# Expert stage of a two-block layer: gathered rows replaced by dense products over both tables

## The chip, the cores and the metric

One core of a Trainium2 chip runs the whole program. The metric is the device time of one execution in microseconds; times of the kernel before are the median of three runs. TensorE is called PE in the profile, its weight loads PEld, VectorE DVE, ScalarE ACT, GpSimd POOL, and SP is the queue that issues most transfers.

## What is computed

Two transformer-like blocks over 256 tokens of width 1024, all in f32. The part that the change rewrites is the expert layer at the end of the first block. It has 16384 experts, each with one row of 1024 numbers in a table u and one in a table v (64 MB a table). For each token, 8 heads pick 16 experts each by products of two half keys, 128 experts in all, with softmax gates:

```python
def chunk(args):
    xc, ec, gc = args
    u = expert_u[ec]
    act = jax.nn.gelu(jnp.einsum('cd,ced->ce', xc, u).astype(jnp.float32))
    return jnp.einsum('ce,ced->cd', gc * act, expert_v[ec])
```

The expert index is i1 * 128 + i2, where i1 and i2 are the winners of the two half-key searches. Before this layer stand modulation vectors, an attention with three branches, a short convolution and the output projection; behind it a residual add, a norm, and the whole second block (attention, a gated delta rule, gates, output projection, norm).

## The kernel before

The tokens are two tiles of 128. Every engine has its own instruction queue, written out in order by the Python program (`PE`, `V`, `A`, `G`, `SP` are TensorE, VectorE, ScalarE, POOL and SP); an engine runs its queue strictly in that order and each entry names the earlier results that it waits for (`after`). Nearly every instruction is recorded under one line, L87, so groups are told apart by the tiles that they name. PSUM has eight banks of 128x512, handed out in turn by `ps.take()`. Weights of 1024x512 come in 2 MB loads into four slots `W`, in the order of the list `plan` (line 160 on): `next_w` takes the next, `done_w` releases it and asks for the block four places on.

`attn_mm(a)` is the output projection of token tile a (16 products of 512 columns), `attn_add(a)` its residual add on VectorE, `queries(a)` the norm, the transposes (`norm_T`), the query projection (64 products of 128 columns), and, back in token order, the row `tok2[:, a]` that the gathers need. `key_scores` gives the half-key scores; `route(a)` (line 780) picks top 16 by repeated max operations on VectorE, in tiles `RT`, `PT` and `acc`, and ends in the expert index `idx` and the gate `gw`. It is a generator: its instructions are put into VectorE's queue a few at a time, between those of the gathers.

The expert stage is the loop `for m in range(17)` (line 959). Block m is 16 experts of one head of a token tile. For each expert slot s, POOL issues an indirect transfer that fetches for each of the 128 tokens its own row of table u (512 KB) into one of 14 buffers of `AR`. VectorE multiplies it with the token's row and sums into `av`. Sixteen such sums go through gelu and the gates to `wv`. One block later POOL fetches the v rows of the same slots; ScalarE makes a diagonal matrix of the 128 weights, and TensorE multiplies it with the rows into two PSUM banks `E[a]` (two products of 512 columns for each slot). That is 2 x 256 fetches. In between stand `mod_row(3, n)` (a gate row of the modulation, 16 products of 512 columns in all), the route of tile 1, and from m = 8 on for token tile 0, whose sums are complete by then: `x2(0)` (gate, residual, norm), the second block's norm and transposes, `qk_project` (q and k, four times 8 products of 512 columns) and `rope`. After the loop the same is done for tile 1, and the second block goes on with `rope_turn`, the projections of tile 1 and of v, and so on.

## Time and profile before

| | us |
|---|---|
| median of three runs | 1529.59 |
| lowest and highest | 1529.15, 1543.69 |
| span of the profiled execution | 1593.7 |
| mean granted TensorE clock in it | 0.944 |

The span is from the first instruction to the last in one execution with the profiler on. Busy time of an engine is that of its compute instructions; a matmul's end is modelled and overlaps the next one's start a little, so for dense stretches the step from one start to the next tells the cost. An f32 product shows as two MATMUL records, and two weight loads. "Idle before" is what stood ahead of the instructions of a group, with the releaser that ended it.

### The profile page before, as it was taken

To read this page: it belongs to the slowest core of one execution; us is meant where nothing else is said; L and a number is where in the kernel's file an instruction comes from. 1 tells how busy PE (TensorE), PEld (TensorE's weight loads), DVE (VectorE), ACT (ScalarE), POOL (GpSimd) and SP (SyncE) were. 2 spreads that over 40 slices of the span, in tenths; PEclk is the share of its full clock that TensorE was granted. 3 is DMA by queue.
4 is the path that set the end of the run, shared out by engine and by line. 5 is a ranking of instruction groups with operands and counts; after the bars stand their busy time and mean duration, and the time that the engine had idled before them with its cause. 6 is when DMAs were issued, how large, how long until landed. Compare 5 with 4: busy or idle time off the path is not lost.

```text
span 1593.7 us, 12966 instructions
## 1 busy us (share of the span) xinstructions
PE 1283.0 (81%) x4744; PEld 769.3 (48%) x4744; DVE 750.8 (47%) x1673; ACT 335.6 (21%) x725; POOL 660.3 (41%) x541
## 2 busy tenths in 40 slices
PE   5899878757767777638887877779998698999896
PEld 1697536622322232213333322244676478999783
DVE  2223544778775854435444444320367764441211
ACT  1031211121110121102111111120486452111101
POOL 0787000767777776766777777710000000000000
PEclk9889788889999999988999999989999999999998
DMA  9775300999999999997999999934432131114120
GB/s 341 268 265 211 106 14 1 347 404 370 367 353 370 368 387 388 373 357 256 362 374 361 375 346 394 366 144 160 162 117 92 53 106 53 53 53 157 55 106 26
DMA packets 127690, 376.94 MB, mean 237 GB/s; under 512 B 10403, under 2 KB 12620, under 8 KB 127564
## 3 DMA queue, kind: packets, MB, share of 16 engines
q0 software_dynamic: 73728, 268.47, 44.6%
q1 hardware_dynamic: 52112, 103.46, 18.1%
q10 hardware_dynamic: 1788, 4.19, 0.8%
q8 instruction: 38, 0.62, 0.2%
q14 instruction: 24, 0.20, 0.0%
HBM read 375.02 MB, written 1.06 MB: 236 GB/s over the span
## 4 chain that ended last, share of the span: by engine, by line
PE 41%; DVE 17%; DMA 15%; POOL 13%; issue 7%; ACT 5%; another core or an unknown queue 2%; SPq 0%; DVEq 0%; ACTq 0%
PE ps L87 41%; POOL AR L87 13%; DMA AR<-in_pv,idx 9%; DVE AR L87 7%; DMA AR<-in_pu,idx 3%; ACT L87 2%; DMA W<-in_w_mod 2%; DVE acc L87 2%; DVE RT L87 2%; DVE tok L87 1%; ACT AR L87 1%; DVE hT L87 1%; DVE junk L87 1%; DVE PT L87 1%
## 5 line engine op out<-in xcount | busy, mean ns | idle before, releaser
L87 PE MATMUL ps<-AR,acc 128*128 128x512 f32 x1024 | 502.5, 626 | 173.2 <-DMA AR<-in_pv,idx 116.9
L87 DVE CUSTOM_DVE_ANT_0 AR<-AR,tok 128x1024 f32<-128x1024 f32 x256 | 312.1, 1222 | 263.0 <-DMA AR<-in_pu,idx 227.0
L87 PEld LDWEIGHTS ps<-AR,acc 128*128 128x128 f32 x1024 | 183.6, 194 | 490.3 <-DMA AR<-in_pv,idx 246.3
L87 POOL DMA_INDIRECT AR<-in_pu,idx x256 | 269.5, 1053 | 215.6 <-DVE hred L87 124.9
L87 POOL DMA_INDIRECT AR<-in_pv,idx x256 | 298.8, 1167 | 109.2 <-issue 57.8
L87 PE MATMUL ps<-hT,W 128*128 128x256 f32 (+2 forms) x1504 | 320.7, 372 | 7.0 <-issue 2.4
L87 PEld LDWEIGHTS ps<-hT,W 128*128 128x128 f32 (+1 forms) x1504 | 270.2, 196 | 50.7 <-issue 12.8
L87 ACT ACTIVATE acc<-K,wv 128x128 f32<-128x128 f32 x256 | 86.9, 393 | 227.9 <-PE ps L87 137.0
L87 ACT ACT_TABLE_LOAD x87 | 111.6, 1283 | 16.7 <-issue 15.2
L87 PE MATMUL ps<-W,hT 128*128 128x512 f32 (+3 forms) x288 | 95.1, 487 | 0.0
L87 PE MATMUL ps<-K,tok 128*128 128x128 f32 x128 | 28.2, 390 | 52.7 <-DVE tok L87 52.7
L87 PEld LDWEIGHTS ps<-W,hT 128*128 128x128 f32 x288 | 48.0, 190 | 45.1 <-issue 45.0
L87 POOL TENSOR_TENSOR W<-W,st 128x4096 f32<-128x4096 f32 x6 | 42.1, 7014 | 61.7 <-DMA W<-in_w_mod 61.7
L87 ACT ACTIVATE wv<-av 128x16 f32<-128x16 f32 x16 | 3.4, 215 | 264.3 <-issue 172.8
L87 PE MATMUL ps<-AR,W 128*128 128x256 f32 x256 | 57.1, 379 | 0.0
L87 PEld LDWEIGHTS ps<-K,tok 128*128 128x128 f32 x128 | 22.7, 205 | 62.5 <-DVE tok L87 53.3
L87 ACT ACTIVATE AR<-ps 128x512 f32<-128x512 f32 (+5 forms) x53 | 24.2, 471 | 128.9 <-PE ps L87 128.9
L87 PEld LDWEIGHTS ps<-AR,W 128*128 128x128 f32 x256 | 48.2, 190 | 6.3
L87 PE MATMUL ps<-AR 64*64 64x30 f32 (+4 forms) x288 | 47.6, 312 | 1.0 <-DVE rowb L87 1.0
L87 ACT ACTIVATE PT<-ps 128x512 f32<-128x512 f32 x34 | 19.8, 591 | 118.2 <-PE ps L87 118.2
L87 PEld LDWEIGHTS ps<-AR 64*64 64x64 f32 (+2 forms) x288 | 39.0, 197 | 9.1 <-issue 4.9
L87 POOL TENSOR_TENSOR W<-W 128x2048 f32<-128x2048 f32 (+1 forms) x12 | 41.7, 3478 | 0.9
(200 smaller groups left out, 1035.9 us busy)
## 6 DMA issues: line engine op xcount, KB each, us to landing
W<-in_w_in SPq DMA_DIRECT2D x25, 2048.0 KB, 7.8
W<-in_w_mod SPq DMA_DIRECT2D x12, 2048.0 KB, 16.2
W<-in_w_out SPq DMA_DIRECT2D x2, 2048.0 KB
W<-in_wq SPq DMA_DIRECT2D x2, 2048.0 KB, 10.5
AR<-in_pu,idx POOLq DMA_INDIRECT x256
AR<-in_pv,idx POOLq DMA_INDIRECT x256
W<-in_wba SPq DMA_DIRECT2D x2, 2048.0 KB, 7.9
W<-in_wbb SPq DMA_DIRECT2D x2, 2048.0 KB, 7.8
```

Of the source, the lines that this page charges most:

```text
L87: ins = f(*args, **kw)
```

## The change

The routing stays, but for its cut: `route` now puts all its instructions out in three goes, for four heads at a time, and keeps i1 and i2 (`i12`) rather than the index. In place of the gathers:

- Both tables are laid out on the host in 64 blocks of 1 MB, each of a pair of blocks of 128 experts. SP's queue loads block after block into a ring of four buffers. The ring lies where weight slots 0 and 1 are.
- `act_pair(p)`: products of the u block with all 256 tokens, 2 x 8 products of 256 columns into one bank; ScalarE's gelu writes the result (expert by token) into `held`, 128 x 256 numbers for each partition. It covers the gather buffers and, by the time that they are needed, slots 2 and 3 and the tiles `tok2`, `acc`, `mixT`, `PT`, `RT`.
- The gates of a token over all experts are a 128 x 128 matrix, the product of two one-hot matrices of 128 columns (i2, made by POOL; i1 times the gate, made by VectorE) over the 128 chosen. `one_hots(g)` makes them for four tokens, `gate_mm(g)` multiplies (4 products of 128 columns), `gate_spread(g)` multiplies them into those experts of `held` that are there, and ScalarE copies the rest, for which `gate_pair` multiplies later. Two such groups go with each pair from 30 to 61.
- The second table, from pair 28 on and round: for each block 2 x 2 x 2 products of 512 columns, `held` times v, into four banks.

Also moved: `attn_mm(1)` ahead of `queries(0)`, `mod_row(3, n)` ahead of `attn_add(1)`, the transposes back to token order are gone, and tile 0's `x2`, norm, transposes and q and k projections now follow the whole expert stage. Weight blocks 22 to 25 of the plan are loaded late: 22 and 23 in the second table's pass, 24 and 25 after its last product. Rows 0 and 1 of `rowb` are loaded after the gate products.

```diff
+M_W23 = M_AR + 14 * D
+M_TOK = M_W23 + 2 * 4096
+M_ACC = M_TOK + 2 * D
...
         def done_w(i, tok):
-            load_w(i + NSLOT, [tok])
+            if not L1 - NSLOT <= i < L1:
+                load_w(i + NSLOT, [tok])
...
-        for r in range(4):
+        for r in (2, 3):
             SP.dma(nc.sync.dma_start, s_row, rowb[:, r, :], rows[r, :].partition_broadcast(P))
         t_row = SP.dma(nc.sync.dma_start, s_row, abb[:, :], ab[0, :].partition_broadcast(P))
...
-            for k4 in range(2):
-                b = ps.take()
-                for kk in range(4):
-                    t = PE(tr, b.t[:, kk * 128:kk * 128 + 128], hT[:, 4 * k4 + kk, c], ident, after=b.old + t_h)
-                e = A(act, tok2[:, a, k4 * 512:k4 * 512 + 512], b.t[:, :], ACT.Copy, after=[t, t_xn])
-                b.free = [e]
-                t_h2[a].append(e)
+            t_h2.extend(t_h)
+            t_tp2.append(t_xn)
...
-        attn_add(0, attn_mm(0))
+        ob0, ob1 = attn_mm(0), attn_mm(1)
+        attn_add(0, ob0)
         queries(0)
-        RT = sb("RT", [P, 6 * 256])
+        t_g2 = [mod_row(3, n) for n in range(2)]
+        attn_add(1, ob1)
+        queries(1)
...
-        ob1 = attn_mm(1)
-        routes = [route(0, kb, [stage[7, "O"]])]
-        while (0, 0) not in t_idx or (0, 0) not in t_gw:
-            advance(routes[0], 1)
-        attn_add(1, ob1)
-        queries(1)
...
-        def fetch(table, a, s):
-            n = gn[0] % NGB
-            gn[0] += 1
-            return n, G.dma(nc.gpsimd.indirect_dma_start, gsem[n], GB[:, n, :], None, table,
-                            bass.IndirectOffsetOnAxis(ap=idx[:, a, s:s + 1], axis=0),
-                            after=slot_free[n] + [t_idx[a, s // 16]])
...
+        ring = [M[:, r * 2048:r * 2048 + 2048] for r in range(4)]
+        rsem = [dsem(f"s_r{r}") for r in range(4)]
+        turn_v = [*range(28, NPAIR), *range(28)]
+        t_ring = []
+        def fetch(i, after):
+            if i < 2 * NPAIR:
+                src = pu[i, :, :] if i < NPAIR else pv[turn_v[i - NPAIR], :, :]
+                t_ring.append(SP.dma(nc.sync.dma_start, rsem[i % 4], ring[i % 4], src, after=after))
+        for i in range(4):
+            fetch(i, [t_g2[i // 2]])
+        ones2 = held.rearrange("p (c t) -> p c t", t=S)
+        t_act, t_prod, t_store, t_one = {}, {}, {}, {}
...
+        def act_pair(p):
+            b = ps.take()
+            u = ring[p % 4].rearrange("p (k e) -> p k e", k=8)
+            for cc in range(2):
+                for k in range(8):
+                    t = PE(mm, b.t[:, cc * 256:cc * 256 + 256], u[:, k, cc * 128:cc * 128 + 128], hT[:, k, :],
+                           start=(k == 0), stop=(k == 7), after=b.old + [t_ring[p]] + t_h2)
+            fetch(p + 4, [t])
+            src = b.t[:, :].rearrange("p (c t) -> p c t", c=2)
+            dst = ones2[:, 2 * p:2 * p + 2, :]
+            n = min(8 * max(p - P0, 0), S)
+            b.free = []
+            if n < S:
+                e = A(act, dst[:, :, n:], src[:, :, n:], ACT.Gelu_apprx_tanh, after=[t] + t_tp2)
+                b.free.append(e)
+            if n:
+                e = A(act, src[:, :, 0:n], src[:, :, 0:n], ACT.Gelu_apprx_tanh, after=[t])
+            t_act[p] = e
+            return b, src, dst, n
+        def gate_pair(p, b, src, dst, n):
+            if n:
+                t_prod[p] = V(tt_, dst[:, :, 0:n], src[:, :, 0:n], dst[:, :, 0:n], MUL,
+                              after=[t_act[p], t_store[2 * (n // 8) - 1]])
+                b.free.append(t_prod[p])
+        def one_hots(g):
+            h = hot[g % 3]
+            for j in range(4):
+                c = 4 * g + j
+                t2_ = G(nc.gpsimd.tensor_scalar, h[:, 0, j, :], i128, i2T[:, c:c + 1], None, ALU.is_equal,
+                        after=hotfree[g % 3] + t_turned)
+                t = V(ts_, h[:, 1, j, :], i128, i1T[:, c:c + 1], gT[:, c:c + 1], ALU.is_equal, MUL,
+                      after=hotfree[g % 3] + t_turned)
+            t_one[g] = [t, t2_]
+        def gate_mm(g):
+            b = ps.take()
+            h = hot[g % 3]
+            for j in range(4):
+                t = PE(mm, b.t[:, j * 128:j * 128 + 128], h[:, 0, j, :], h[:, 1, j, :], start=True, stop=True,
+                       after=b.old + t_one[g])
+            hotfree[g % 3] = [t]
+            return b, t
+        def gate_spread(g, b, t):
+            c = 2 * (P0 + g // 2 + 1)
+            src = b.t[:, :].rearrange("p (t c) -> p c t", t=4)
+            dst = ones2[:, :, 4 * g:4 * g + 4]
+            t = V(tt_, dst[:, 0:c, :], src[:, 0:c, :], dst[:, 0:c, :], MUL, after=[t, t_act[P0 + g // 2]])
+            b.free = [t]
+            t_prod["g"] = t
+            if c < P:
+                t = A(act, dst[:, c:, :], src[:, c:, :], ACT.Copy, after=[t])
+                b.free = [t]
+            t_store[g] = t
+        def turn_route(a):
+            b = ps.take()
+            for n, src in enumerate((i12[:, 0, :], i12[:, 1, :], gw[:, a, :])):
+                t = PE(tr, b.t[:, n * 128:n * 128 + 128], src, ident, after=b.old + [t_i12[a], t_gw[a]])
+            c = slice(a * 128, a * 128 + 128)
+            e = A(act, junk[:, 512:1024].rearrange("p (c t) -> p c t", c=2)[:, :, c],
+                  b.t[:, 0:256].rearrange("p (c t) -> p c t", c=2), ACT.Copy, after=[t] + t_jx[-1:])
+            e = A(act, gT[:, c], b.t[:, 256:384], ACT.Copy, after=[t])
+            b.free = [e]
+            return t, e
+        routes = route(0, kb, [stage[7, "O"]], [])
+        kb1 = []
+        for p in range(P0):
+            act_pair(p)
+            if p == 5:
+                next(routes)
+                kb1.append(key_scores(1, 0))
+            if p == 13:
+                next(routes)
+                next(routes)
+                t_turn0, e0 = turn_route(0)
+                kb1.append(key_scores(1, 1))
+                routes = route(1, kb1, [t_gw[0]], [t_turn0])
+            if p == 20:
+                next(routes)
+            if p == P0 - 2:
+                next(routes)
+                next(routes)
+                t_turned = [e0, turn_route(1)[1]]
+        one_hots(0)
+        one_hots(1)
+        for p in range(P0, NPAIR):
+            pair = act_pair(p)
+            gs_ = [g for g in (2 * (p - P0), 2 * (p - P0) + 1) if g < NPAIR]
+            banks = [gate_mm(g) for g in gs_]
+            for g, (b, t) in zip(gs_, banks):
+                if g + 2 < NPAIR:
+                    one_hots(g + 2)
+                gate_spread(g, b, t)
+            gate_pair(p, *pair)
+        s_row2 = dsem("s_row2")
+        for r in range(2):
+            t_row2 = SP.dma(nc.sync.dma_start, s_row2, rowb[:, r, :], rows[r, :].partition_broadcast(P),
+                            after=hotfree[0] + hotfree[1])
+        E = [[ps.take(), ps.take()] for _ in range(2)]
+        for q, p in enumerate(turn_v):
+            v = ring[q % 4].rearrange("p (c d) -> p c d", c=2)
+            for cc in range(2):
+                for a in range(2):
+                    for n in range(2):
+                        t = PE(mm, E[a][n].t[:, :], ones2[:, 2 * p + cc, a * 128:a * 128 + 128],
+                               v[:, cc, n * 512:n * 512 + 512], start=(q == 0 and cc == 0),
+                               stop=(q == NPAIR - 1 and cc == 1),
+                               after=E[a][n].old + [t_ring[NPAIR + q], t_act[p], t_prod["g"], t_store[NPAIR - 1]]
+                               + ([t_prod[p]] if p in t_prod else []))
+            fetch(NPAIR + q + 4, [t])
+            if q == 15:
+                load_w(L1, [t])
+                load_w(L1 + 1, [t])
+        load_w(L1 + 2, [t])
+        load_w(L1 + 3, [t])
+        t_pelast = t
...
-        for m in range(17):
-            last = None
-            for s in range(16):
-                if m < 16:
-                    a, h = blocks[m]
-                    q = h * 16 + s
-                    n, t = fetch(pu, a, q)
-                    last = V(ttr, GB[:, n, :], GB[:, n, :], tok2[:, a, :], 1.0, 0.0, MUL, ADD, av[:, a, q:q + 1],
-                             after=[t] + t_h2[a])
-                    slot_free[n] = [last]
-                    t_last0 = last if a == 0 else t_last0
-                    t_last1 = last
-                if m >= 1:
-                    a, h = blocks[m - 1]
-                    q = h * 16 + s
-                    n, t = fetch(pv, a, q)
-                    if q == 0:
-                        E[a] = [ps.take(), ps.take()]
-                    d = dn[0] % NDG
-                    dn[0] += 1
-                    td = A(act, dg[:, d, :], ident, ACT.Copy, scale=wv[:, a, q:q + 1], after=[t_w[m - 1]] + dg_free[d])
...
-                        routes = [route(1, [key_scores(1, 0), key_scores(1, 1)], [t_idx[0, 7], t_gw[0, 7]])]
-            if m in (4, 5):
-                t_g2.append(mod_row(3, m - 4))
-            if m < 16:
-                a, h = blocks[m]
-                c = slice(h * 16, h * 16 + 16)
-                t = A(act, wv[:, a, c], av[:, a, c], ACT.Gelu_apprx_tanh, after=[last])
-                t_w[m] = V(tt_, wv[:, a, c], wv[:, a, c], gw[:, a, c], MUL, after=[t, t_gw[a, h]])
-            if m == 8:
-                assert (1, 7) in t_gw
-                t_x2[0] = x2(0, e, [])
-                t_xb = norm_x(0, st[:, 16:17], [t_x2[0]], tok2, [t_last0])
-                t_, t_tp = norm_T((0,), tok2, [t_xb], PV[:, V_PRE:V_PRE + 8], None, [])
-                t_hb.append(t_)
-            if m in (9, 10):
-                qk_project("qk"[m - 9], 0, 0, [t_tp, t_gw[1, 7]])
...
-        t_x2[1] = x2(1, t_pelast, t_rot["k", 0])
-        t_xb = norm_x(1, st[:, 17:18], [t_x2[1]], tok2, [t_last1])
-        t_, t_tp = norm_T((1,), tok2, [None, t_xb][1:], PV[:, V_PRE:V_PRE + 8], None, [])
+        t_x2[0] = x2(0, t_pelast, [])
+        t_xb0 = norm_x(0, st[:, 16:17], [t_x2[0]], tok2, [t_pelast])
+        t_, t_tp0 = norm_T((0,), tok2, [t_xb0], PV[:, V_PRE:V_PRE + 8], None, [])
         t_hb.append(t_)
+        t_x2[1] = x2(1, t_pelast, [t_xb0])
+        t_xb = norm_x(1, st[:, 17:18], [t_x2[1]], tok2, [t_pelast])
+        for n in range(2):
+            for kind in "qk":
+                qk_project(kind, 0, n, [t_tp0])
+        t_, t_tp = norm_T((1,), tok2, [t_xb], PV[:, V_PRE:V_PRE + 8], None, [])
+        t_hb.append(t_)
+        rope("q", 0, [t_xb])
+        rope("k", 0, t_rot["q", 0])
         t_hball = t_hb[0] + t_hb[1]
         at[0] = 0
...
+    pu = a["peer_u"][0].reshape(NPAIR, 2 * P, 8, P).transpose(0, 3, 2, 1).reshape(NPAIR, P, 2 * D)
+    pv = a["peer_v"][0].reshape(NPAIR, 2, P, D).transpose(0, 2, 1, 3).reshape(NPAIR, P, 2 * D)
```

## Rows read from the trace of the kernel before

**Rows 1.** The page, parts 1 and 3: engines' busy time; the gathers' queue.
```profile
PE 1283.0 (81%) x4744; PEld 769.3 (48%) x4744; DVE 750.8 (47%) x1673; ACT 335.6 (21%) x725; POOL 660.3 (41%) x541
q0 software_dynamic: 73728, 268.47, 44.6%
```
**Rows 2.** Busy by stretches: length; PE, PEld, DVE, ACT, POOL; clock, DMA share, GB/s.
```profile
330.00:1060.00 730.00, 548.02 (x1160) 206.01 (x1160) 389.94 (x884) 108.00 (x296) 530.71 (x483) 0.96 0.96 360
```
**Rows 3.** Groups by shape, whole span (busy, mean ns, idle before); POOL's first gather.
```profile
L87 PE MATMUL ps<-AR,acc 128*128 128x512 f32 x1024 | 502.5, 626 | 173.2 <-DMA AR<-in_pv,idx 116.9 <-issue 37.0 <-ACT acc L87 19.0
L87 DVE CUSTOM_DVE_ANT_0 AR<-AR,tok 128x1024 f32<-128x1024 f32 x256 | 312.1, 1222 | 263.0 <-DMA AR<-in_pu,idx 227.0 <-issue 35.9
...
L87 POOL DMA_INDIRECT AR<-in_pu,idx x256 | 269.5, 1053 | 215.6 <-DVE hred L87 124.9 <-issue 69.2 <-DVE av L87 10.9
...
280.25 1.11 POOL L87 DMA_INDIRECT AR<-in_pu,idx  x1 [124.88 <-DVE hred L87]
```
**Rows 4.** TensorE in order of time, first output projection to key scores.
```profile
229.63 15.67 PE L87 MATMUL ps<-W,mixT 128*128 128x512 f32 x32 [4.64 <-DVE modc L87]
249.30 1.97 PE L87 MATMUL ps<-K,tok 128*128 128x128 f32 x8 [4.00 <-DVE tok L87]
252.26 9.99 PE L87 MATMUL ps<-hT,W 128*128 128x128 f32 x64 [0.99 <-ACT hT L87]
...
264.57 7.41 PE L87 MATMUL ps<-hT,W 128*128 128x128 f32 x64
272.67 1.71 PE L87 MATMUL ps<-PT,mixT 64*128 64x128 f32 x16 [0.69 <-ACT mixT L87]
```
**Rows 5.** TensorE in order of time, end of the gathers and what follows.
```profile
1030.53 29.75 PE L87 MATMUL ps<-AR,acc 128*128 128x512 f32 x68 [0.58 <-issue]
1068.75 3.67 PE L87 MATMUL ps<-K,tok 128*128 128x128 f32 x16 [8.47 <-DVE tok L87]
...
1073.73 41.37 PE L87 MATMUL ps<-W,hT 128*128 128x512 f32 x96
```
**Rows 6.** TensorE in dense stretches, in order of time; one weight-load group by shape.
```profile
1427.26 1.95 PE L87 MATMUL ps<-tok,junk 128*128 128x128 f32 x16
1429.04 1.95 PE L87 MATMUL ps<-tok,PT 128*128 128x128 f32 x16
...
1434.29 7.07 PE L87 MATMUL ps<-hT,W 128*128 128x256 f32 x32
1441.19 7.07 PE L87 MATMUL ps<-AR,W 128*128 128x256 f32 x32
...
1553.80 27.70 PE L87 MATMUL ps<-W,acc 128*128 128x512 f32 x64 [1.60 <-DVE acc L87]
...
L87 PEld LDWEIGHTS ps<-W,acc 128*128 128x128 f32 x64 | 12.1, 190 | 16.8 <-issue 16.8
```
**Rows 7.** Busy time of a dense stretch, columns as in rows 2.
```profile
1434.00:1480.00 46.00, 46.00 (x264) 41.81 (x263) 7.17 (x11) 7.31 (x23) 0.00 (x0) 1.00 0.39 138
```
**Rows 8.** Busy time of the routing tile RT alone; PE, PEld, DVE, ACT.
```profile
240.00:1060.00 820.00, 0.00 (x0) 0.00 (x0) 118.36 (x472) 0.00 (x0) 0.95 0.91 343
```
**Rows 9.** The page, part 6: weight loads, KB each, us to landing.
```profile
W<-in_w_in SPq DMA_DIRECT2D x25, 2048.0 KB, 7.8
```
**Rows 10.** Groups by shape, whole span: nearest rows to the new small operations.
```profile
L87 POOL TENSOR_TENSOR W<-W 128x2048 f32<-128x2048 f32 x6 | 27.6, 4602 | 0.5
L87 POOL TENSOR_TENSOR mixT<-W 128x512 f32<-128x512 f32 x4 | 5.6, 1397 | 0.3
L87 POOL MEMSET AR<- 128x8 f32 x1 | 0.1, 106 | 0.0
...
L87 DVE TENSOR_SCALAR rowb<-rowb,sm 128x128 f32<-128x128 f32 x8 | 2.3, 287 | 0.3
L87 DVE TENSOR_TENSOR AR<-ps,bd 128x512 f32<-128x512 f32 x4 | 2.8, 692 | 7.7 <-PE ps L87 7.7
L87 ACT ACTIVATE PT<-ps 128x512 f32<-128x512 f32 x34 | 19.8, 591 | 118.2 <-PE ps L87 118.2
```

More of the change, by code:

```diff
@@ L777, in build, with route @@
         i16 = K[:, K_I16:K_I16 + 16]
-        t_idx, t_gw = {}, {}
-        def route(a, banks, hold):
+        t_gw = {}
+        t_i12 = {}
+        def route(a, banks, hold, hold_i):
             t_sel = hold
-            for h0, nh in ((0, 2), (2, 2), (4, 4)):
+            for h0, nh in ((0, 4), (4, 4)):
                 bs, t = banks[h0 // 4]
@@ L870, in route @@
-                yield
-                t_gn = V(tt_, g3, g3, hr.unsqueeze(2).to_broadcast([P, nh, 16]), MUL, after=[t])
-                for h in range(h0, h0 + nh):
-                    t_idx[a, h], t_gw[a, h] = t_new, t_gn
-                t_sel = t_sel + [t_new, t_gn]
-                yield
+            g3 = gw[:, a, :].rearrange("p (h s) -> p h s", h=8)
+            t = V(tt_, g3, t163[:, :, :], t163[:, :, 0:1].to_broadcast([P, 8, 16]), SUB, after=t_sel)
+            t_e = A(act, gw[:, a, :], gw[:, a, :], ACT.Exp, after=[t])
@@ L877, in advance @@
+            t = V(red, hred[:, a, :], g3, AX, ADD, after=[t_e])
+            t = V(rec, hred[:, a, :], hred[:, a, :], after=[t])
+            t_gw[a] = V(tt_, g3, g3, hred[:, a, :].unsqueeze(2).to_broadcast([P, 8, 16]), MUL, after=[t])
+            yield
         def advance(gen, n):
@@ new lines, in build @@
+        for i in range(4):
+            fetch(i, [t_g2[i // 2]])
+        ones2 = held.rearrange("p (c t) -> p c t", t=S)
+        t_act, t_prod, t_store, t_one = {}, {}, {}, {}
+        i1T, i2T = junk[:, 512:768], junk[:, 768:1024]
+        gT = sb("gT", [P, S])
+        i128 = K[:, K_I128:K_I128 + P]
+        hot = [rowb[:, r, :].rearrange("p (c t i) -> p c t i", c=2, t=4) for r in range(3)]
+        hotfree = [t_g1 + t_x1[1] for _ in range(3)]
+        def act_pair(p):
[17 more added lines that the diff above has]
+            return b, src, dst, n
@@ L920, in x2 @@
             t = rms(X[:, a, :], D, st[:, 14 + a:15 + a], [t])
-            return V(stt, X[:, a, :], X[:, a, :], st[:, 14 + a:15 + a], R_LNF, MUL, MUL, after=[t, t_row])
-        blocks = [(a, h) for a in range(2) for h in range(8)]
+            return V(stt, X[:, a, :], X[:, a, :], st[:, 14 + a:15 + a], R_LNF, MUL, MUL, after=[t, t_row2])
         rot = {("q", 0): tok2[:, 0, :], ("k", 0): acc[:, 1, :], ("q", 1): tok2[:, 1, :], ("k", 1): acc[:, 0, :]}
```

165 lines of the change are left out of this document (54 added, 111 removed).

## The prediction

> **What bounds the kernel now.** I read the page from the top. The first part says that no engine is busy for the whole span [rows 1]: an average over stages, so the stages were looked at next, by stretches. In the stretch of the gathers [rows 2] the 16 DMA engines are busy 0.96 of the time at 360 GB/s, TensorE 548.0 of 730 us, VectorE 389.9. The queue of the gathers moved 268.47 MB [rows 1], which is 512 fetches of 128 rows of 4 KB. The groups by shape say who waits: TensorE's products with gathered rows stand 173.2 us idle, 116.9 of them for gathered rows of the second table, VectorE's row products 263.0 us, 227.0 of them for rows of the first [rows 3]. So the stage ends when the rows are in. TensorE's last product with them ends at 1030.53 + 29.75 = 1060.3 [rows 5]. After that the kernel is a chain of TensorE, VectorE and ScalarE with hardly any DMA in it, and the change leaves that part as it is, but for its first few products.
>
> **What a product costs.** Every f32 product stands in the trace as two MATMUL records, a transpose as one. In dense stretches 32 records of 256 columns step by 1441.19 - 1434.29 = 6.90 us, 0.431 us a product; 16 records of 128 columns step by 1429.04 - 1427.26 = 1.78, 0.223 us a product; 64 records of 512 columns take 27.70 us, less about 0.17 for the last one's drain, 0.860 us a product [rows 6]. The granted clock was 1.00 in the first of these stretches [rows 7], which is the level of 2.4 GHz, so nothing is left to gain there.
>
> **The dense stage.** First table: 64 pairs of expert blocks, each 2 x 8 products of 256 columns, the very shape of the 32 records above: 64 x 6.90 = 441.6 us. Gate products: 256 (one per token) of 128 columns: 256 x 0.223 = 57.1. Second table: 64 x 2 x 2 x 2 = 512 products of 512 columns: 512 x 0.860 = 440.3 (439.6 by the last step of the records). Key scores of the second token tile (two blocks of 16 records, 1.64 each [rows 4]) 3.3, six turning transposes 0.7. Sum 942.3 us of TensorE alone; I take that for the stage, if TensorE never waits in it. What has to hide below it:
> - Tables: 1 MB per 6.9 us is 152 GB/s, against the 360 of the gathers [rows 2]. A load of 2 MB lands in 7.8 us [rows 9], and the ring of four asks for each block 20 us ahead. Hidden; it would cost only if the loads ran at less than half of what they do.
> - Routing: VectorE's work on the routing tile is 118.4 us for both token tiles [rows 8], some 59 each. The first must be through when TensorE, in order, comes to its transposes behind pair 13, 97 us after the stage's start, the second behind pair 28, 200 us after it. The next late thing would be TensorE itself, by whatever is missing. Hidden with 35 us to spare.
> - ScalarE: one activation of 128x512 for each pair (0.59 [rows 10]) and the copies of gates, under 1 us: under 2 of 6.9, with room for table loads.
> - One-hots and spreading, pairs 30 to 61: TensorE's own time there is 6.90 + 8 x 0.223 = 8.68 us a pair. VectorE has 8 tensor_scalar of 128x128 (0.287 each), two spreads and one product of 128x512 (0.692 each) [rows 10]: 4.4 us. POOL has 8 compares of 128x128, of which the trace has no row. From below 0.106 (8 columns), from above 1.397 (512 columns) [rows 10]; the step to 2048 columns (4.602) gives 2.1 ns a column and so 0.6 at 128, a line from the 8 columns gives 0.4. I take 0.5: 4.0 us a pair, hidden; at the upper end 11.2 a pair, not hidden (a rival below). The spread reads PSUM with a stride, of which I have no better row.
>
> A rule speaks against this. In rows, VectorE's and POOL's one-hots together are 2.3 + 4.0 = 6.3 us of 8.68 a pair, so even if they took turns the sum stays. The Trainium skill, "SBUF — State Buffer", section "Who interferes with whom", says that VectorE's tensor_scalar in its two-port mode and a POOL instruction lock each other out for a whole instruction. No row of before has the two side by side. By that rule with POOL's price at its upper end a pair would need 13.5 us and the kernel 1982 in place of 1909.
>
> **Ahead of the stage.** Before: first output projection 229.63 to 245.3, transposes at 249.30, query products 9.99 and 7.41, key scores 1.71 twice, and so on [rows 4]. After, TensorE's order is: both output projections, queries of tile 0, the gate row of w_mod (16 products, 13.7), queries of tile 1, the pairs. Tile 0: 245.3 + 13.7 (second projection) = 259.0; transposes 1.0 and eviction 1.0; then twice 7.4 + 0.7 + 1.6: 280.4. The gate row: 294.1, its add on VectorE (0.7) 294.8. Behind that add in VectorE's queue stand the residual adds of tile 1, and TensorE waits for them: four adds of 0.7 and the norm (the 4.00 us ahead of 249.30 less two adds, 2.6 [rows 4]) take it to 300.2; transposes and eviction 1.97 + 0.99, queries 9.99 + 7.4 (the first products at the lower clock, as in rows 4): 320.6. The stage then ends at 320.6 + 942.3 = 1262.9, that is 202.6 later than 1060.3.
>
> **Behind the stage.** In before the second normalization, the transposes and the projections of q and k for token tile 0 ran while gathers were awaited; only tile 1 stood behind. From 1060.3 the chain takes 8.47 us to the transposes and to 1073.73 for the next products, 13.4 in all [rows 5]. After, tile 0 comes first: 8.47, then 1.97 + 0.99, then four projections of 8 products of 512, 27.5 us, then tile 1's transposes with their eviction 2.0 (tile 1's own norm lies under the 27.5), the rotations of q and k, 12 small VectorE operations of 0.287 = 3.4, and transposes 0.9. That is 45.2, or 31.8 more. Two of the four weight blocks can only be asked for when the last table block is consumed; two loads of some 7.8 us, one behind the other, land at 16, and TensorE needs them at 8.5 + 3 + 13.7 = 25. Hidden.
>
> **Sum.** 1593.7 + 202.6 + 31.8 = 1828.1 us of span. Removed with the gathers: 512 issues on POOL (1.05 us each for the first table [rows 3]), 256 VectorE row products, 256 diagonals on ScalarE, 1024 MATMUL records; they lay beside one another in the 780 us from the first issue at 280.25 [rows 3] to 1060.3, whose end is compared above, and aren't subtracted again.
>
> **Span and time.** The profiled execution's span, 1593.7, is 64.1 us over the median of 1529.59. Where those 64 us sit decides what to set against the runs. The DMA engines were nearly full all through the gathers [rows 2]; a product at 512 columns in 0.43 us a record at full clock can't be faster in an undisturbed run. So I put all 64 into the gathers (0.125 us each of 512), which the change removes, and expect after's time at its span: 1828.
>
> **The rivals.**
> - *The 64 us are spread over the span.* Then the part that both kernels share, 1593.7 - 780 = 814 us, is 64.1 x 814 / 1593.7 = 33 shorter in undisturbed runs: 1795. For it: the DMA engines are at work outside the gathers too. Against: much of the rest is product-bound, and in the stretch of [rows 7] at the full clock. Chance 0.15.
> - *POOL's compares bound pairs 30 to 61.* At 1.397 each, 11.2 a pair against 8.68, 32 pairs: +81, 1909. It decides from 1.09 us each. For it: no row at 128 columns. Against: POOL's rows grow with the columns. Chance 0.10.
> - *The clock falls.* At the lower level (1.2 GHz) the first queries' 64 records of 128 columns took 9.99 against 7.41, the first few of them slow [rows 4]; a product stream at that level costs twice. In the first product alone: +442, 2270. Against: it fell only after TensorE had stood idle, and here it never does. Chance 0.04.
> - *The other side: a dense stream goes faster than the rows.* If a record cost only its weight load (0.190 [rows 6]) once the queue is full, the second table would cost 1024 x 0.190 = 195 (-245) and the first 2048 x 0.190 = 389 (-53): 1530, no change. It takes a saving of 299 out of 882 to decide. Against: 64 and 32 records on end already step at 0.43 and 0.216. Chance 0.03: 0.02 no change, 0.01 faster. The Trainium skill, "TensorE: Matmul & The Clock Gate", section "Back-to-back issue gap", has such a rule: it gives some 131 ns for a product of 512 columns in a real stream. By it the second table's 1024 records would be 134 us and the kernel 1522. The rows of this trace, at 430, contradict it.
>
> **How the numbers follow.** Forecast as summed, 0.68; the rivals 0.15, 0.10, 0.04, 0.03. The time is that of the likeliest, 1828. Its own range is 1810 to 1850 (the order ahead and behind, some 10 us each, and a few us around the span). The range down to 1785 takes in the spread of the 64 us, up to 1885 most of the way to POOL's bound. A measurement of this kernel can't tell less than about 1%; slower by over 1% has 0.97, same 0.02, faster 0.01.
>
> **What would show it.** In after: about 7168 MATMUL records of the expert stage, TensorE busy throughout at a granted clock of 1.00 between about 320 and 1263; DMA near 150 GB/s there; POOL's compares well under 1.09 us; transposes about 8.5 us behind the last product; the next chain 32 us longer than before. Wrong if TensorE has steady idle time in pairs 30 to 61 (named after POOL or VectorE), or if pairs take less than 6.9 us; and if after's time lies as far under its span as before's does, the 64 us weren't the gathers'.

## The result, and the profile after

The kernel after takes 1846.6 us (median of 4 executions, 1845.85 to 1847.62), the kernel before 1534.5 on the same chip; the ratio is 1.202, 95% interval 1.197 to 1.207. That is 19 us above the 1828 predicted, inside the predicted range and inside the forecast's own. The page of after:

```profile
span 1844.8 us, 17497 instructions
PE 1721.7 (93%) x7294; PEld 1226.7 (66%) x7294; DVE 547.8 (30%) x1456; ACT 290.9 (16%) x599; POOL 243.4 (13%) x285
PE 83%; DVE 10%; ACT 4%; DMA 2%; issue 1%; SPq 0%; DVEq 0%; ACTq 0%
M<-in_pv SPq DMA_DIRECT2D x64, 1024.0 KB, 4.9
```

The third line is the chain that ended last: 83% of it is TensorE. Against [rows 1] TensorE's busy share went from 81% to 93%, with 2550 records more (the stage's own products are 2048 + 512 + 1024 = 3584 records, and the 1024 with gathered rows are gone); the gathers' queue is gone, and each 1 MB table block lands in 4.9 us. The stretches, with the columns of [rows 2]:

```profile
540.00:780.00 240.00, 240.00 (x1322) 217.07 (x1321) 93.93 (x295) 34.77 (x108) 128.72 (x219) 1.00 0.35 123
830.00:1280.00 450.00, 444.15 (x1046) 198.35 (x1044) 6.07 (x9) 2.07 (x3) 0.00 (x0) 1.00 0.45 160
```

In [rows 2] the DMA engines were busy 0.96 of the time and TensorE 0.75. Now TensorE is busy all of the gated pairs and of the second table's pass, at a granted clock of 1.00, the level of 2.4 GHz, and the DMA engines are busy 0.35 and 0.45. The bound has gone from the transfers to the products, and the products are more work than the transfers were. TensorE in order of time (start, us, idle before and its releaser):

```profile
361.50 1.71 PE L102 MATMUL ps<-M 64*128 64x128 f32 x16
363.14 55.52 PE L102 MATMUL ps<-hT,M 128*128 128x256 f32 x256
421.94 0.66 PE L102 MATMUL ps<-K,M 128*128 128x128 f32 x2 [3.28 <-DVE gw L102]
...
422.75 3.09 PE L102 MATMUL ps<-M 64*128 64x128 f32 x16
425.77 104.73 PE L102 MATMUL ps<-hT,M 128*128 128x256 f32 x480
533.79 0.66 PE L102 MATMUL ps<-K,M 128*128 128x128 f32 x2 [3.28 <-DVE gw L102]
...
534.45 15.13 PE L102 MATMUL ps<-hT,M 128*128 128x256 f32 x64
549.42 1.95 PE L102 MATMUL ps<-rowb 128*128 128x128 f32 x16
...
558.12 1.95 PE L102 MATMUL ps<-rowb 128*128 128x128 f32 x16
...
1259.82 14.32 PE L102 MATMUL ps<-M 128*128 128x512 f32 x33
1282.62 1.97 PE L102 MATMUL ps<-K,M 128*128 128x128 f32 x8 [8.47 <-DVE M L102]
1285.40 30.55 PE L102 MATMUL ps<-M,hT 128*128 128x512 f32 x64 [0.81 <-ACT hT L102]
...
1321.42 23.77 PE L102 MATMUL ps<-M,hT 128*128 128x512 f32 x55
```

A gated pair takes 558.12 - 549.42 = 8.70 us (8.68 by the sum), and nowhere in the pairs does TensorE wait for a table block or for a one-hot. It waits twice, 3.28 us each, for the gates `gw`, and behind each of these waits the products are slow: behind the first, the 16 key-score records take 3.09 where the same number took 1.71 at 361.50; behind the second, 64 records of 256 columns take 15.13, and 13.98 later on, at 820.70. The first product of the second table starts at 834.52. Who waited for whom, TensorE over the stage and VectorE in 300 to 540 (us in total, times, longest), and ScalarE in order of time around the first of the two waits:

```profile
PE ps L102 <- DVE gw L102: 6.6, 2, 3.3
...
DVE hred L102 <- ACT gw L102: 120.8, 2, 64.2
...
418.69 0.60 ACT L102 ACTIVATE M<-ps 128x512 f32<-128x512 f32 x1 [6.31 <-PE ps L102]
419.31 1.28 ACT L102 ACT_TABLE_LOAD   x1
420.60 0.31 ACT L102 ACTIVATE gw<-gw 128x128 f32<-128x128 f32 x1
```

VectorE had done its part of the first routing some 62 us before the gates were wanted and then stood still, 64.2 us in all, for the exponential of `gw`. That one stands in ScalarE's queue behind the gelu of pair 13, since `route` gives out its last piece there, and so it can't run before pair 13's products are through, which is when TensorE wants the gates already.

Where the 16.7 us of span above the sum lie (1844.8 against 1828.1):

| part | by the sum | measured | difference |
|---|---|---|---|
| start of the stage (361.50 less six pairs of 6.90) | 320.6 | 320.1 | -0.5 |
| first table, gates, key scores, transposes, to 834.52 | 502.7 | 514.4 | +11.7 |
| second table, 834.52 to 1274.14 | 439.6 | 439.6 | 0.0 |
| behind the stage, to 1321.42 | 45.2 | 47.3 | +2.1 |
| from there to the end (before: 1073.73 to 1593.7) | 520.0 | 523.4 | +3.4 |

The last 1.8 us of the 18.6 between 1846.6 and 1828 lie around the span.

### The profile page after: what moved, and what is told of

The parts are those of the page before. It is cut to its first block, busy times and chain, and to the rows that moved or that the text cites. A ratio compares the mean times of both kernels' runs of the same rounds, so it can differ in the third digit from the quotient of the medians.

```text
span 1844.8 us, 17497 instructions
## 1 busy us (share of the span) xinstructions
PE 1721.7 (93%) x7294; PEld 1226.7 (66%) x7294; DVE 547.8 (30%) x1456; ACT 290.9 (16%) x599; POOL 243.4 (13%) x285
## 4 chain that ended last, share of the span: by engine, by line
PE 83%; DVE 10%; ACT 4%; DMA 2%; issue 1%; SPq 0%; DVEq 0%; ACTq 0%
PE ps L102 83%; DVE M L102 7%; ACT L102 2%; ACT M L102 2%; DMA M<-in_w_mod 2%; DVE hT L102 1%; DVE sm L102 0%; ACT rowb L102 0%; DMA M<-in_w_in 0%; DVE rowb L102 0%; DVE cst_ L102 0%; DVE X L102 0%; DVE tiny L102 0%; ACT hT L102 0%; ACT st L102 0%
## 5 line engine op out<-in xcount | busy, mean ns | idle before, releaser
L102 PE MATMUL ps<-hT,M 128*128 128x256 f32 (+2 forms) x3552 | 772.5, 378 | 3.2 <-DVE M L102 1.3
L102 PEld LDWEIGHTS ps<-hT,M 128*128 128x128 f32 (+1 forms) x3552 | 658.3, 193 | 98.8 <-issue 7.6
L102 PE MATMUL ps<-M 128*128 128x512 f32 (+6 forms) x2426 | 700.7, 449 | 21.2 <-DMA M<-in_rel 7.3
L102 PEld LDWEIGHTS ps<-M 128*128 128x128 f32 (+3 forms) x2426 | 391.9, 193 | 323.4 <-issue 295.5
L102 ACT ACTIVATE M<-ps 128x512 f32<-128x512 f32 (+20 forms) x277 | 124.1, 457 | 861.3 <-PE ps L102 791.3
L102 POOL TENSOR_SCALAR rowb<-K,M 128x128 f32<-128x128 f32 x256 | 151.3, 610 | 505.4 <-ACT gT L102 378.4
L102 DVE TENSOR_TENSOR M<-ps,M 128x512 f32<-128x512 f32 (+34 forms) x147 | 68.9, 491 | 321.3 <-PE ps L102 308.8
L102 PE MATMUL ps<-M,hT 128*128 128x512 f32 (+3 forms) x288 | 97.5, 498 | 0.8 <-ACT hT L102 0.8
L102 DVE TENSOR_SCALAR rowb<-K,M,gT 128x128 f32<-128x128 f32 x256 | 77.2, 365 | 1.6 <-ACT gT L102 1.6
L102 PE MATMUL ps<-rowb 128*128 128x128 f32 x512 | 62.3, 275 | 0.0
## 6 DMA issues: line engine op xcount, KB each, us to landing
M<-in_w_out SPq DMA_DIRECT2D x2, 2048.0 KB, 10.3
M<-in_wq SPq DMA_DIRECT2D x2, 2048.0 KB, 10.3
```

The source lines that it names most:

```text
L102: ins = f(*args, **kw)
```

## Experiments

A time without a number of executions beside it is that of one execution.

**The exponentials four pairs earlier.** Same instructions; the last piece of each token tile's routing is put into the queues four pairs ahead of its transposes.

```diff
+            if p == 9:
+                next(routes)
+                next(routes)
             if p == 13:
-                next(routes)
-                next(routes)
                 t_turn0, e0 = turn_route(0)
...
+            if p == P0 - 6:
+                next(routes)
+                next(routes)
             if p == P0 - 2:
-                next(routes)
-                next(routes)
```

> Edit: the last step of the routing of each token tile (the exponential on ScalarE and the gates) is put into the queues four pairs earlier (behind pair 9 and pair 24), TensorE's turning transposes stay behind pairs 13 and 28. My theory: TensorE's two waits of 3.28 us there come from ScalarE's queue order (the exponential stands behind the activation of pair 13, or 28, so it can't run before TensorE is through with that pair), and each idle time costs some 1.3 us more at the lower clock behind it, three times. Expected: both waits gone, 6.6 + about 4 = 10.5 us less than 1846.6, about 1836. Rival: the routing on VectorE is itself late there (my estimate of 59 us for each tile too small); then the waits stay and the time is 1846 to 1847.

Measured: 1833.9 us, 12.7 less than after (10.5 were expected). TensorE's rows of this kernel:

```profile
418.88 0.38 PE L102 MATMUL ps<-K,M 128*128 128x128 f32 x2
...
420.94 103.87 PE L102 MATMUL ps<-hT,M 128*128 128x256 f32 x480
524.64 0.38 PE L102 MATMUL ps<-K,M 128*128 128x128 f32 x2
```

The two rows of transposes have no wait ahead of them, and the second table's first product starts at 823.88, so that from the stage's start (320.5) to there it is 503.4 us, where the sum said 502.7. That is 11.0 of the 11.7 us. The waits themselves were 6.6 of them. The rest goes with a lower clock after them, as the busy time of short stretches shows, the first two of after (ahead of the first wait, and behind it), the third of this experiment at nearly the same place; columns as in [rows 2]:

```profile
410.00:418.00 8.00, 8.00 (x39) 7.04 (x38) 0.00 (x0) 0.60 (x1) 0.00 (x0) 1.00 0.38 133
422.00:432.00 10.00, 10.00 (x44) 8.60 (x45) 9.96 (x66) 1.83 (x3) 0.00 (x0) 0.72 0.09 35
```
```profile
420.00:430.00 10.00, 10.00 (x55) 8.82 (x54) 9.79 (x38) 0.72 (x2) 0.00 (x0) 1.00 0.39 129
```

In 10 us behind the wait the granted clock is 0.72, a mean of time at 1.2 and at 2.4 GHz, and 44 records are there. Counted from the same point of its stream, 418.94 to 428.94, this experiment has 57 at a clock of 1.00. So a wait of 3.28 us cost 5.5 on the mean of the two (some 6 the first, some 5 the second). The other 1.7 of the 12.7 us aren't shown to come from the edit: the stage began 0.4 later here, from the second table's end to the next projections it is 0.5 less than in after, and 1.6 less from there to the end.

**POOL's compares made twice.** Each compare is followed by the same one again: 16 a pair in place of 8.

```diff
-                t2_ = G(nc.gpsimd.tensor_scalar, h[:, 0, j, :], i128, i2T[:, c:c + 1], None, ALU.is_equal,
-                        after=hotfree[g % 3] + t_turned)
+                for _ in range(2):
+                    t2_ = G(nc.gpsimd.tensor_scalar, h[:, 0, j, :], i128, i2T[:, c:c + 1], None, ALU.is_equal,
+                            after=hotfree[g % 3] + t_turned + ([t2_] if _ else []))
```

> Edit: each compare of POOL (the one-hot of i2) is made twice into the same place, all else as in the changed kernel. POOL's compare took 0.610 us there, eight of them 4.9 us of the 8.69 us of a gated pair. Theory A, POOL and VectorE run beside each other: 16 compares are 9.8 us, over 8.69, so the pair's period becomes 9.8 and 32 pairs cost some 35 us more, about 1882. Theory B, the two shut each other out: 9.8 + 8 x 0.365 = 12.7 us a pair, 128 us more, about 1975. Rival, POOL has more slack than its rows say: 1847.

Measured: 1889.8 us, +43. TensorE in order of time, and the one-hot instructions in the stretch of the gated pairs (durations: lowest, median, highest, in ns):

```profile
604.13 1.05 PE L102 MATMUL ps<-rowb 128*128 128x128 f32 x8
606.55 1.13 PE L102 MATMUL ps<-rowb 128*128 128x128 f32 x8 [1.37 <-POOL rowb L102]
...
614.43 1.05 PE L102 MATMUL ps<-rowb 128*128 128x128 f32 x8
...
L102 POOL TENSOR_SCALAR rowb<-K,M x477: 593/601/721, 534.3 to 840.0; 128x128 f32<-128x128 f32 x159
...
L102 DVE TENSOR_SCALAR rowb<-K,M,gT x244: 329/340/460, 534.1 to 835.5; 128x128 f32<-128x128 f32 x122
```

A pair takes 614.43 - 604.13 = 10.30 us, which is 16 x 0.60 and a little for the hand-over: POOL is now the bound, and the wait is named after it. The eight VectorE compares (8 x 0.34 = 2.7 us) lie beside POOL's. If the two took turns, a pair would need at least 9.6 + 2.7 = 12.3 us. The Trainium skill, "SBUF — State Buffer", section "Who interferes with whom", has VectorE's tensor_scalar in its two-port mode and a POOL instruction shut each other out; these instructions of 128x128 f32 didn't. The trace doesn't say in which mode VectorE's ran, so this speaks of these instructions and not of the rule. The point from which POOL decides, 1.09 us a compare, fits: at 0.60 a compare TensorE never waited for one, at twice 0.60 it does, and the pairs grew by 1.6 us, 0.9 by the sum and the rest in the hand-over.

**Every table block loaded twice.** To see how far the table loads are from mattering. The second load of a block waits for the first one.

```diff
-                t_ring.append(SP.dma(nc.sync.dma_start, rsem[i % 4], ring[i % 4], src, after=after))
+                t = SP.dma(nc.sync.dma_start, rsem[i % 4], ring[i % 4], src, after=after)
+                t_ring.append(SP.dma(nc.sync.dma_start, rsem[i % 4], ring[i % 4], src, after=[t]))
```

> Edit: each 1 MB block of both tables is loaded twice, the second time after the first has landed; the traffic of the stage doubles to some 304 GB/s. Theory: transfers are hidden below TensorE with a ring of four, two loads of 4.9 us one behind the other are 9.8 of 20.7 us of lead: 1847, within 3 us. Rival: the stage leans on transfers or on memory traffic, so TensorE gets waits for blocks: 1 MB more in a pair at the rate of the gathers (360 GB/s) is 2.9 us, over 128 blocks up to 370 us more.

Measured: 1882.7 us, +36: a miss. The first table's pass has no wait; the second's has. TensorE's waits and SP's over the stage, TensorE in order of time, the second pass by stretch (length; PE; clock, DMA share, GB/s), and one issue of SP's queue:

```profile
PE ps L102 <- DMA M<-in_pv: 23.1, 42, 11.2
...
SPq L102 <- DMA M<-in_pv: 428.3, 64, 11.4
...
952.33 7.13 PE L102 MATMUL ps<-M 128*128 128x512 f32 x16 [0.19 <-DMA M<-in_pv]
959.66 7.13 PE L102 MATMUL ps<-M 128*128 128x512 f32 x16 [0.20 <-DMA M<-in_pv]
...
985.43 15.01 PE L102 MATMUL ps<-M 128*128 128x512 f32 x30 [11.17 <-DMA M<-in_pv]
...
840.00:1320.00 480.00, 447.60 (x1010) 0.98 0.74 282
...
962.48 1.06 SPq L102 DMA_DIRECT2D M<-in_w_in  x2
```

The transfers had room: 282 GB/s at a DMA share of 0.74. The queue had none. SP's queue is in order, and in it now stands a wait for the first load's landing, 428.3 / 64 = 6.7 us a block, with the next block's issue behind it. A block then comes every 959.66 - 952.33 = 7.33 us, and TensorE wants one every 6.87. What I had reckoned was bandwidth; what bound was the time to land, once for every block, with only the second load of the block before it under way beside it. The stall of 11.17 us comes once, and not by chance: at 962.48 the queue issues the two weight loads of 2 MB (blocks 22 and 23 of the plan) that stand behind the 16th block of this pass, and the table blocks behind them come that much later. The pass took 473.4 us in place of 439.6, which is nearly all of the 36. In after, where nothing in the queue waits for a landing, TensorE has no wait for a table block, the weight loads included. (The experiment thus measured an added wait more than the added traffic, and says of the traffic only that 282 GB/s are to be had beside the products.)

**Half of the second table's products.** The expectation says which part is left out.

```diff
-            for cc in range(2):
+            for cc in range(1):
                 for a in range(2):
                     for n in range(2):
```

> The changed kernel with half of the second table's products left out: of each block only the first 128 experts are multiplied, all blocks are still loaded. Theory, TensorE's products are the stage: 256 products of 512 columns less, 256 x 0.859 = 219.9 us, 1626.7. Rival, something that every block costs anyway is near the bound: a block would then take more than 3.44 us (1 MB at the 360 GB/s of the gathers is 2.9 us, which doesn't bind; at 284 GB/s, the rate of the twice-loaded tables, 3.7 us, it would, and the time would be 1643).

Measured: 1630.3 us, 216.3 less than after, where the rows had 219.9. TensorE in the second table's pass, and the weight loads in SP's queue:

```profile
831.93 68.83 PE L102 MATMUL ps<-M 128*128 128x512 f32 x160
905.37 153.74 PE L102 MATMUL ps<-M 128*128 128x512 f32 x352 [4.61 <-DMA M<-in_pv]
...
887.43 1.06 SPq L102 DMA_DIRECT2D M<-in_w_in  x2
```

The pass takes 905.37 + 153.74 - 831.93 = 227.2 us, where half of 439.6 is 219.8. The 7.4 between them are one wait of 4.61 for a late block and the products behind it: 160 records ahead of it step by 0.430, as in [rows 6], the 352 behind it by 0.436 on the mean (+2.3; granted clock 0.74 from 905 to 915). The pass had begun 2.6 us earlier than in after, which gives part of it back. The late block again stands behind the two weight loads, 4 MB issued at 887.43. So the second table costs what its records say, and at 1 MB in 3.44 us (305 GB/s) the loads still hold, but for that one place.

**Where before's 64 us lay.** The kernel before, profiled once more.

> The kernel before, unchanged, for a second profiled execution. The first had a span of 1593.7 while the other executions took 1529 to 1544. Theory (as in the prediction): the 64 us lie in the gathers, so in an execution of some 1536 TensorE's last product with gathered rows ends near 1000, not 1060, and what stands behind it is as long as in the first profile (533 us). Rival: they are spread, so that the part behind is some 20 us shorter too.

Measured: 1544.4 us with a span of 1542.5, that is 51.2 under the span shown of before. TensorE at the end of the gathers, and the stretch of the gathers:

```profile
978.71 29.45 PE L87 MATMUL ps<-AR,acc 128*128 128x512 f32 x68 [0.59 <-DMA AR<-in_pv,idx]
1016.63 3.40 PE L87 MATMUL ps<-K,tok 128*128 128x128 f32 x16 [8.47 <-DVE tok L87]
...
330.00:1008.00 678.00, 538.52 (x1158) 203.07 (x1156) 387.39 (x875) 107.38 (x288) 511.19 (x481) 0.98 0.99 386
```

The last product with gathered rows ends at 1008.2, against 1060.3 [rows 5], 52.1 earlier, of which 2.7 had been gained ahead of the gathers. From there to the end it is 534.3 us, and 533.4 in the execution shown. So 49.4 of the 51.2 us lie in the gathers, which ran at 386 GB/s in place of 360 [rows 2]. The part that both kernels share hardly differs between these two executions. That the gathers vary is measured; what makes them vary isn't, nor whether their bytes or their number bound them: of the kernel before with rows of half the length there is no time.

**The same dense stage with its products in bf16.** Both tables, `hT` and `held` are rounded to bf16 after the load, a table block by ScalarE in the first pass and by VectorE in the second. A block's place in the ring is asked for again once it is rounded, and the second table is taken from pair 56 on and round. The results are less precise than those of before and after.

```diff
+        hTb = W[3].rearrange("p k n -> p (k n)")[:, 0:1024].bitcast(BF).rearrange("p (k t) -> p k t", k=8)
+        t_hTb = V(cpv, hTb, hT[:, :, :], after=t_h2 + t_qp[1])
...
-                    t = PE(mm, b.t[:, cc * 256:cc * 256 + 256], u[:, k, cc * 128:cc * 128 + 128], hT[:, k, :],
-                           start=(k == 0), stop=(k == 7), after=b.old + [t_ring[p]] + t_h2)
+                    t = PE(mm, b.t[:, cc * 256:cc * 256 + 256], u[:, k, cc * 128:cc * 128 + 128], hTb[:, k, :],
+                           start=(k == 0), stop=(k == 7), after=b.old + [t_cast, t_hTb])
```

> Edit: the dense products of both tables are made in bf16 rather than f32 (the rest of the layer stays f32): ScalarE casts each u block, VectorE each v block, activations and gates are held in bf16, and the ring asks for the next block when the cast is done. So it computes the expert products with less precision. Theory: the f32 products are what the dense stage costs (882 of 954 us). At one record in place of two and half the time a column, a pair of u takes some 1.7 us and of v some 1.7 us, so the bounds become transfers (1 MB in 2.8 us) or the cast (some 2 us), and in the 32 gated pairs VectorE and POOL (about 5 us). Sum: 30 x 2.9 + some 25 of waiting for the routing + 32 x 5 + 2 x 2.9 + 64 x 2.9 = 463 in place of 954: about 1355, below the kernel before (1534). Rival: the stage is bound by something that doesn't depend on the products (transfers, casts, order): over 1534. If the casts are slower than that (4 us each) 64 x 1.1 x 2 = 140 more, about 1500.

Measured: 1339.8 us. Taken again it was 1340.2 (4 executions), ratio to before 0.872, interval 0.869 to 0.875:

> The kernel of e4_bf16 once more, with rounds, beside e9_bf16_pool on the same chip, so that both have an interval: 1340 +- 4, ratio to before about 0.872, TensorE's two waits for the gates near 20 and 16 us as before. If the single run of e4_bf16 was off, it shows here.

The second table's pass in the first of these runs, TensorE in order of time, then VectorE's and ScalarE's rounding of the blocks (busy, mean ns, idle before):

```profile
615.77 1.90 PE L103 MATMUL ps<-M 128*128 128x512 bf16 x8 [0.58 <-DVE M L103]
618.26 1.90 PE L103 MATMUL ps<-M 128*128 128x512 bf16 x8 [0.59 <-DVE M L103]
...
L103 DVE CAST M<-M 128x2048 bf16<-128x2048 f32 x64 | 78.3, 1226 | 89.1 <-DMA M<-in_pv 87.8 <-PE ps L103 1.3
...
L103 ACT ACTIVATE M<-M 128x2048 bf16<-128x2048 f32 x64 | 122.3, 1913 | 2.0 <-DMA M<-in_pu 1.8
```

A bf16 product is one record, not two, and a shorter one, so a block is 8 products in 1.90 us where it was 16 records in 6.87. Now a block takes 618.26 - 615.77 = 2.49 us, and VectorE's rounding waits for the load: 1 MB in 2.49 us is 421 GB/s, so the second pass is bound by the transfers again, but by 64 MB read once in order and not by gathered rows. This shows what made the change slow: not the dense form, but two records of 0.430 for each f32 product of 512 columns. It isn't a like comparison with before, which computes in f32; no run has the gathers with tables in bf16.

**The same with the gates earlier.** Routing brought forward, so that the gates are ready at pair 14, and the spreading of tile 0 started there in the place of pair 30 (`P0 = 14`); tile 1's follows 16 pairs later.

```diff
-P0 = 30
+P0 = 14
...
+            if p == P0 - 1:
+                t_turn0, t_turned[0] = turn_route(0)
                 routes = route(1, kb1, [t_gw[0]], [t_turn0])
...
+            if p == P0 + 15:
+                t_turned[1] = turn_route(1)[1]
```

> Edit on top of the kernel with bf16 products: gates of the first token tile are spread from pair 14 on (before the second tile is routed), those of the second from pair 30; the second tile's routing stands between them in VectorE's queue, and each exponential four or more pairs ahead of the transposes that need it. The expert products are in bf16, as there. Theory: there TensorE waited 36.3 us for the two routings and the 32 gated pairs ran at 4.9 us, the time of POOL's eight compares (8 x 0.610). With the gates begun while the second routing runs, those 4.9 us a pair start at about 372 rather than 437, and VectorE's 50 us of routing lie beside them in part: first product through at some 570 in place of 597, about 1312. Rival: VectorE is the bound in pairs 14 to 29 (routing 50 us + 16 x 4.4 of gates = 120 us against POOL's 78), and what is won in front is lost there: 1335 to 1340.

Measured: 1384.1 us (4 executions, 1381.7 to 1387.4), ratio 0.901, interval 0.897 to 0.905: a miss by 72 us, and 44 slower than with the gates late. TensorE's waits in the stage:

```profile
PE ps L103 <- DVE M L103: 85.1, 67, 11.4
...
PE ps L103 <- DVE rowb L103: 39.5, 2, 28.2
```

The one-hots and spreads of tile 0 now stand in VectorE's queue behind pieces of tile 1's routing, some 59 us of work in large pieces, and TensorE waits 28.2 us at once for a one-hot, up to 492.5. VectorE is busy 27.6 of the 28.5 us from 464.0 to there, nearly all of it with the routing's max and index operations. I had added up the engines' work and forgotten the queue's order, as in the sum on record.

**One rounding moved to POOL.** The bf16 kernel with the gates late is the start again. In it VectorE had stood 18.15 us in front of the rounding of `hT`, with the routing behind it.

```diff
-        t_hTb = V(cpv, hTb, hT[:, :, :], after=t_h2 + t_qp[1])
+        t_hTb = G(nc.gpsimd.tensor_copy, hTb, hT[:, :, :], after=t_h2 + t_qp[1])
```

> The kernel of e4_bf16 (both dense streams with tables and activations rounded to bf16) with one change: the rounding of hT, which stood ahead of the routing in VectorE's queue, is done by POOL. In e4_bf16 VectorE waited 18.15 us for it behind ScalarE, and TensorE then waited 20.42 us for the first token tile's gates and 15.91 for the second's. If the in-order queue is the cause, the first routing starts some 18 us earlier and TensorE's first wait shrinks to a few us; the second routing starts earlier as well, but TensorE comes to it earlier too, so that its wait stays near 16. POOL's rounding of 128x2048 (no row yet; 2 to 5 us, by POOL's 4.6 us for a product of that shape in rows 10) holds up the first pair by 1 to 4 us. 1339.8 - 18 + 2 = 1324, ratio to before about 0.862. Rival: VectorE's wait was for something that the routing needs too (the key scores' bank, the queries), so nothing moves: 1340 to 1343.

Measured: 1322.4 us (4 executions, 1321.5 to 1325.5), ratio 0.861, interval 0.858 to 0.864; the fastest kernel here. TensorE's two rows at the gates, first in the bf16 kernel run beside it, then in this one, and POOL's rounding:

```profile
377.33 0.66 PE L103 MATMUL ps<-K,M 128*128 128x128 f32 x2 [21.36 <-DVE gw L103]
432.91 0.66 PE L103 MATMUL ps<-K,M 128*128 128x128 f32 x2 [15.97 <-DVE gw L103]
```
```profile
361.60 0.66 PE L103 MATMUL ps<-K,M 128*128 128x128 f32 x2 [4.24 <-DVE gw L103]
417.18 0.66 PE L103 MATMUL ps<-K,M 128*128 128x128 f32 x2 [15.94 <-DVE gw L103]
...
322.05 1.89 POOL L103 CAST M<-hT 128x2048 bf16<-128x2048 f32 x1 [166.81 <-ACT M L103]
```

The first wait fell by 17.1, the second stayed, since both VectorE and TensorE come to it earlier, and the run fell by 17.8. This time the order of the queue was in the expectation, and it came out within 2 us.

## Why the prediction was right, and where it wasn't

- **The time**: 1846.6 for 1828, 1% over. The mechanism was the forecast's, TensorE's products one after another. Most of the distance is one step, the routing; that it was small enough to stay in the forecast's range of 1810 to 1850 is luck, since that range was made for the order ahead and behind the stage, and these came out within 0.5 and 2.1 us.
- **"What a product costs" and "The dense stage"**: right. The second table took 439.6, as the last step of the records had it. Without the two waits the first table with gates and key scores takes 503.4 where the sum said 502.7.
- **"Routing: hidden with 35 us to spare"**: this step failed. It counted VectorE's work and asked when that is through; it left out the one instruction of the chain that another engine does. The exponential stood in ScalarE's queue behind the gelu of pair 13 and again of pair 28. That put ScalarE's table load and exponential and VectorE's three small operations on TensorE's path: twice 3.28 us and the clock behind it. Taken out, the stage up to the second table was 11.0 us shorter (12.7 in the time). The code had shown it: `route` gives out its last piece just ahead of the transposes, `act_pair(13)` before it.
- **Tables**: right. No wait for a block in after; a block landed in 4.9 us. "If the loads ran at less than half of what they do" was a fair figure for bandwidth, which the half-table kernel bears out at 305 GB/s, and said nothing of the queue's order, which is what the doubled loads and the blocks behind the weight loads met.
- **One-hots**: POOL's compare is 0.610 on the mean over the whole (median 0.601 in the gated stretch), not 0.5, VectorE's 0.365, not 0.287. Per pair 4.9 and 2.9 us, still under 8.70, so neither mattered. The rival of POOL's bound was the right mechanism at the wrong price; made true by doubling, it came.
- **Rivals**: the 64 us spread over the span is refuted by the second profile of before (49.4 of 51.2 in the gathers). The clock fell only where TensorE had stood idle, and was 1.00 in the stretches from 540 to 1280. The faster stream didn't come: 430 ns a record after 1024 of them in a row, at full clock. The Trainium skill, "TensorE: Matmul & The Clock Gate", section "Back-to-back issue gap", gives some 131 ns for a product of 512 columns in a stream. This trace doesn't agree for f32 (430 ns a record, 860 a product), nor does the bf16 kernel's for bf16 (8 in 1.90 us).
- **Ahead of the stage**: 320.6 against 320.1. **Behind it**: 2.1 short, because the four projections behind the 8.47 us wait begin at the lower clock (30.4 in place of 27.5 us; granted clock 0.69 in their first 10 us), less 0.7 that the rotations took under it. The prediction had taken the slow start into account for the first queries (9.99 and not 7.41) and left it out here. Of the 3.4 us further on, about 1.3 have come by 1475 and another 1.3 about 1600. The same part takes 520.0 and 521.8 us in the two profiles of before, and 521.8 in the run with the exponentials earlier, so about half may be what executions differ by; the cause of the rest stays open.
- **The signs**: "about 7168 MATMUL records of the expert stage" doesn't follow from its own sum, which has 3584 (1792 products, two records each); less the 1024 of the gathered rows and 16 transposes, with six new ones, that is 2550 more, as in the trace. "DMA near 150 GB/s" is 123 in the gated pairs, which are longer, and 160 in the second pass. The next chain is 33.9 longer, not 32.
- **"Span and time"**: after's time stood 1.8 us above its span, so the sum on the span could be set against the runs as it was.

## What to carry to other kernels

A dense product in place of gathers trades transfers for TensorE records, so price it in records first: in f32, 128 experts times 128 tokens cost two records of 0.430 us for each 512 columns, and no hiding elsewhere wins that back; with one shorter record for each product, in bf16 and less precise, the whole kernel came out 13 to 14% shorter than the f32 kernel with the gathers. When work is called hidden, follow its whole chain through every in-order queue that it passes, and write down what stands ahead of each link, not only each engine's sum. On a stream of products at the full clock, reckon a short wait at well over its own length (5.5 us for 3.28 here). Look for what else stands in the queue of a stream of loads: the two late weight loads made TensorE wait once in the half-table kernel, once in the one with doubled loads and once in bf16.

## What the runs showed of the hardware that I had not expected

- A wait of 3.28 us in a stream of products lowered the granted clock in the 10 us behind it to 0.72 and cost about 5.5 us in all, on the mean of two; with the wait gone, it stayed at 1.00 there.
- Two weight loads of 2 MB in the queue of the table blocks made TensorE wait 4.6 us (blocks wanted every 3.44 us), 11.2 us (each block loaded twice) and 11.4 us (bf16, blocks every 2.49 us) for the blocks behind them, and not at all at one block in 6.87 us.
- Blocks of 1 MB read in order came at 421 GB/s in the bf16 kernel, gathered rows of 4 KB at 360 and 386.
- VectorE's and POOL's one-hots of 128x128 f32 ran beside each other: 16 of POOL's (0.60 each) and 8 of VectorE's (0.34 each) in 10.3 us.
- Rounding 128x2048 from f32 to bf16 took 1.226 us on VectorE, 1.89 on POOL, 1.913 on ScalarE: the nearest row beforehand had POOL at 4.6 us for a product of that shape.
